# A two-layer decoder step on one core: four conditioning items of the second layer move from the first layer's route into the sparse attention, whose eight groups are reordered

## What is computed

```python
def ada_mod(c, w, b):
    return jnp.split(jax.nn.silu(c) @ w + b, 6, axis=-1)
...
for i in range(DEPTH):
    sh1, sc1, gt1, sh2, sc2, gt2 = ada_mod(c, w_ada[i], b_ada[i])
    h = modulate(x, norm_mix[i], sh1, sc1)          # rms_norm * (1 + scale) + shift
    m = gla_mixer(h, ...) if i % 2 == 0 else dsa_mixer(h, ...)
    x = x + gt1 * m
    x = x + gt2 * moe_ffn(modulate(x, norm_ffn[i], sh2, sc2), ...)
```

```python
logits = einsum('btkgd,btskd->btkgs', qg, k_sel) * ATT_DH ** -0.5
p = softmax(where(valid, logits + bias, -inf))
o = einsum('btkgs,btskd->btkgd', p, v_sel)
```

## Time and profile before

| | |
|---|---|
| median of 3 runs | 1783.02 us (1780.09 to 1785.51) |
| profiled execution | 1780.96 us |
| its span | 1779.1 us |
| TensorE busy | 1624.9 us (91%), mean granted clock 0.959 |
| VectorE, ScalarE, GpSimd busy | 709.7, 442.2, 166.5 us |
| moved by transfers | 552.37 MB, mean 310 GB/s |

### The profile page before, as it was taken

How to read it: one execution, slowest core, us unless ns; L and a number is a source line. 1 busy time by engine, 2 the same in 40 slices (tenths; PEclk the granted TensorE clock), 3 DMA queues, 4 the chain that set the end, 5 groups by cost and what they waited for, 6 DMA issues and landing times. The chain is left out here.

```text
span 1779.1 us, 30764 instructions
## 1 busy us (share of the span) xinstructions
PE 1624.9 (91%) x11629; PEld 971.7 (55%) x11756; DVE 709.7 (40%) x1909; ACT 442.2 (25%) x985; POOL 166.5 (9%) x229
## 2 busy tenths in 40 slices
PE   5999898899999999999988957798999999999997
PEld 4687475455555555555456744575555555455554
DVE  3123536055333333333332775245733333333334
ACT  2110112122222222222231114131222222222223
POOL 0000300000000000000010424001000000000000
PEclk9899699799999999999999969799999999999999
DMA  9875644999999999999771412065999999999990
GB/s 362 326 259 172 213 148 168 409 385 383 415 416 417 416 414 413 413 416 415 280 297 33 143 49 60 1 239 215 391 402 416 416 416 416 413 416 416 413 396 30
DMA packets 139031, 552.37 MB, mean 310 GB/s; under 512 B 19407, under 2 KB 36637, under 8 KB 104662
## 3 DMA queue, kind: packets, MB, share of 16 engines
q1 hardware_dynamic: 120562, 513.82, 72.5%
q0 software_dynamic: 15392, 34.66, 5.6%
q10 hardware_dynamic: 3012, 3.00, 0.5%
HBM read 562.74 MB, written 8.60 MB: 321 GB/s over the span
## 5 line engine op out<-in xcount | busy, mean ns | idle before, releaser
L1316 PE MATMUL PS<-ring,arena 128*64 128x256 f32 x4288 | 490.7, 382 | 2.5 <-ACT arena L1633 1.5
L1316 PEld LDWEIGHTS PS<-ring,arena 128*64 128x64 f32 x4288 | 304.2, 137 | 182.6 <-issue 41.0
L1340 PE MATMUL PS<-ring,arena 128*64 128x512 f32 x1072 | 259.6, 605 | 1.4 <-ACT arena L1618 1.4
L1540 DVE TENSOR_TENSOR arena<-arena,PS 128x128 f32<-128x128 f32 x134 | 38.6, 288 | 373.9 <-ACT arena L1616 367.9
L1279 PE MATMUL PS<-arena 128*128 128x512 bf16 x669 | 169.4, 384 | 15.1 <-issue 9.2
L1524 DVE TENSOR_SCALAR arena<-arena 128x512 bf16<-128x512 f32 x130 | 62.7, 483 | 256.5 <-ACT arena L1627 256.5
L1626 ACT COPY arena<-PS 64x512 f32<-64x512 f32 x134 | 77.5, 578 | 301.9 <-PE PS L1340 301.9
L1340 PEld LDWEIGHTS PS<-ring,arena 128*64 128x64 f32 x1072 | 65.1, 136 | 120.4 <-issue 104.0
L1646 POOL COPY arena<-arena 128x1 int32 (+1 forms) x71 | 14.5, 204 | 1187.7 <-PE PS L1270 972.0
L1279 PEld LDWEIGHTS PS<-arena 128*128 128x128 bf16 (+1 forms) x796 | 69.6, 99 | 91.5 <-issue 27.7
L1616 ACT ACTIVATE arena<-PS 128x128 f32<-128x128 f32 x134 | 37.2, 278 | 326.4 <-PE PS L1316 326.4
(11 more groups left out here) (482 smaller groups left out, 1618.4 us busy)
## 6 DMA issues: line engine op xcount, KB each, us to landing
ring<-in_moe_w_gate SPq DMA_DIRECT2D x134, 1024.0 KB, 7.8
ring<-in_moe_w_up SPq DMA_DIRECT2D x134, 1024.0 KB, 10.3
ring<-in_moe_w_down SPq DMA_DIRECT2D x134, 1024.0 KB, 15.4
ring<-in_w_ada SPq DMA_DIRECT2D x32, 1152.0 KB
ring<-in_w_ada SPq DMA_DIRECT2D x16, 768.0 KB
ring<-in_gla_w_in SPq DMA_DIRECT2D x8, 1152.0 KB
ring<-in_dsa_w_in SPq DMA_DIRECT2D x6, 1024.0 KB
arena<-in_state_gla POOLq DMA_DIRECT2D x8, 512.0 KB, 5.8
```

The costliest lines, as they stand in the source:

```text
L1316: m = pe.matmul(PS[64 * half:64 * half + 64, 5, 0:256].rearrange("p (g n) -> p g n", g=2), rows[:, k, CAP * b:CAP * b + CAP], gu[:, :, k, ...
L1340: m = pe.matmul(PS[64 * j:64 * j + 64, 7, :], hTt[b][:, kk * CAP:(kk + 1) * CAP], ring[:, s, 2, kk * D + 512 * j:kk * D + 512 * j + 512], ...
```

## The change

Items 4 to 7 of layer 1 leave `pe_route(0)`. Items 4 and 5 have their columns (`pe_late_rows`) behind the first logits of the sparse attention, item 6 behind the transposes of the seventh group, and item 7 at the start of `pe_route(1)`, in place of the seven warming products. Their folds, copies and additions have new functions (`pe_late_fold`, `act_late_rows`, `dve_late`); the rows between lie in `hT` or, for item 7, in its own ring slot. The ring's plan has new slots and a new order: items 5, 6 and 7 are loaded ahead of `w_out`, and the gathers of keys and values use slots that items 4 and 5 had. In the attention, a third buffer for a group, a double one for maximum and sum, a bank of its own for each half-wide group, and a new order: on TensorE logits of `it + 1`, mix of `it - 1`, transposes of `it`; on VectorE scale and mask of `it`, normalising of `it - 1`, maximum of `it`; on ScalarE exponential of `it + 1`, copy of `it`. The prefix sum stands ahead of the transposes of keys and values. The column of a sample's own key is appended to its turned keys by a second copy, so that one product of 257 columns takes the place of one of 256 and one of 1. `Osel` is made on all partitions by 4 operations instead of 16, without the memset.

```diff
-        it_ada[1] = plan(8, at=after)
-        it_ex = [plan(NE, False, at=after[2:] + after[:2] + [it_sh[0][0]]), None]
+        it_ada[1] = plan(4, at=after)
+        it_ex = [plan(NE, False, at=after[1:] + after[:1] + [it_sh[0][0]]), None]
...
+        sa, sb_, sc_, sd = [it_ex[0][u][0] for u in (2, 3, 0, 1)]
+        it_dsa = plan(3, at=[sa, sb_, sc_])
+        hold_raw = hold(sd)
+        it_ada[1] += plan(4, at=[sa, sd, sb_, sc_])
+        hold_k = hold(sa)
+        hold_v = hold(sd)
+        it_dout = plan(2, at=[sb_, sa])
+        it_sh[1] = plan(1, at=[sd])[0]
+        it_ex[1] = plan(NE, False, at=[sb_, sc_, sa, sd])
...
+        def pe_late_rows(i, b):
+            s, _ = it_ada[1][i]
+            item_ready(pe, it_ada[1][i])
+            for t in range(3):
+                for kk in range(2):
+                    for g in range(4):
+                        m = pe.matmul(PS[32 * g:32 * g + 32, b + t // 2, 256 * (t % 2):256 * (t % 2) + 256],
+                                      cT[:, 2 * g + kk, :], wide(s)[:, 2 * g + kk, 256 * t:256 * t + 256],
+                                      start=(kk == 0), stop=(kk == 1), skip_group_check=True)
+            m.then_inc(S("late_rows"), 1)
+            pe.wait_ge(S("late_rows"), i - 3)
+            if i < 7:
+                pe.sem_inc(S(f"slot_used{s}"), 1)
+        def pe_late_fold(i, b, c0):
+            pe.wait_ge(S("mod_rows"), 9 + i)
+            for j in range(6):
+                m = pe.matmul(PS[:, b, c0 + 16 * j:c0 + 16 * j + 9], late_rows(i)[:, j // 2, P * (j % 2):P * (j % 2) + P], K["fold"],
+                              start=True, stop=True)
+            m.then_inc(S("mod_fold"), 1)
...
         def pe_route(l):
-            pe_warm(7)
+            if l:
+                pe_late_rows(7, 5)
+            else:
+                pe_warm(7)
...
             turn_h(0)
+            if l:
+                pe_late_fold(7, 7, 256)
...
-                for i in range(8):
+                for i in range(4):
                     pe_ada_rows(1, i, 3 * (i % 2))
...
+            dve_at(pe, "gteq")
+            pe.matmul(PS[:, 0, 0:2], lowtri, gteq, start=True, stop=True)
+            pe.matmul(PS[:, 0, 2:3], K["m16"], gteq[:, 0:1], start=True, stop=True).then_inc(S("dsa_pe"), 1)
             pe.wait_ge(S("relu"), IH)
...
+            logits(0)
+            pe_late_rows(4, 4)
+            pe_late_rows(5, 6)
+            for it in range(8):
+                if it < 7:
+                    logits(it + 1)
+                if it < 2:
+                    pe_late_fold(4 + it, 5 + 2 * it, 256)
                 if it >= 1:
+                    mix_values(it - 1)
+                if it == 4:
+                    pe.wait_ge(S("mod_T"), 14)
+                turn_probs(it)
+                if it == 6:
+                    pe.wait_ge(S("logit_sb"), 8)
+                    pe_late_rows(6, 0)
+            mix_values(7)
+            pe_late_fold(6, 5, 0)
...
-                    pe.matmul(PS[:, 0, 0:256], Qs[:, Pq, b * P:(b + 1) * P], KTs[b % 4][:, Pq, :], start=(b == 0 and Pq == 0), stop=False, skip_group_check=True)
-                    m = pe.matmul(PS[:, 0, 256:257], Qs[:, Pq, b * P:(b + 1) * P], kT[:, Pq, SEQ + b:SEQ + b + 1], start=False, stop=False, skip_group_check=True)
+                    m = pe.matmul(PS[:, 0, 0:257], Qs[:, Pq, b * P:(b + 1) * P], KTs[b % 4][:, Pq, :], start=(b == 0 and Pq == 0), stop=False, skip_group_check=True)
...
             for it in range(8):
+                masked(it)
+                if it >= 1:
+                    normed(it - 1)
+                largest(it)
+                if it in (1, 2):
+                    dve_late(3 + it, 3 + 2 * it, 256)
+            normed(7)
...
-            dv(dve.memset(Osel, 0.0))
...
             for kv in range(KVH):
+                dst = Osel.rearrange("p (b c d) -> p b c d", b=2, c=2)[:, :, 0]
+                src = PS[:, 1, :].rearrange("p (b k d) -> p k b d", b=2, k=KVH)[:, kv]
...
+            for it in range(8):
+                if it < 7:
+                    exps(it + 1)
+                if it == 4:
+                    mixed_out(0)
+                probs_out(it)
+                if it == 6:
+                    act_late_rows(6, 0)
+            mixed_out(1)
...
             sp_dsa()
+            sp_ada(1, [5, 6, 7])
             sp_dout(0)
             sp_dout(1)
```

More of the change, by code:

```diff
@@ L1478, in dve_route @@
             if l == 0:
-                dve_ada(1)
+                dve_ada(1, range(4))
         def dve_over(l):
@@ L1696, in build @@
         m8 = tk(2, 8)
-        nm, rs, mx = tk(4), tk(4), tk(4)
+        nm, rs = [tk(4) for _ in range(2)], [tk(4) for _ in range(2)]
+        mx = tk(4)
         mxn = tk(4)
@@ L1740, in build @@
         selfP = X2[:, 1300:1308]
[L1741 removed]
+        KTs = [X3[:, 514 * i:514 * i + 514].rearrange("p (q n) -> p q n", q=2) for i in range(4)]
         DC = {k: mrow[:, o:o + w] for k, (o, w) in DSAC.items()}
@@ L1986, in pe_dsa @@
-            pe.wait_ge(S("att_o_sb"), 2)
+                if it >= 2:
+                    pe.wait_ge(S("logit_sb"), it if T else it - 1)
+                r = slice(64 * (kv % 2), 64 * (kv % 2) + 64)
+                for g in range(4):
+                    dst = PS[:, g // 2, 256 * (g % 2):256 * (g % 2) + 2 * P] if T else PS[:, it % 2, P * g:P * g + P]
+                    pe.matmul(dst, qT[r, (kv // 2) * 4 + g, T * P:(T + 1) * P], kT[r, kv // 2, 0:P * (T + 1)],
+                              start=(g % (2 if T else 4) == 0), stop=False, skip_group_check=True)
@@ new lines, in mix_values @@
+            def mix_values(it):
+                T, kv = it // 4, it % 4
+                pe.wait_ge(S("p_T_sb"), it + 1)
+                if it == 4:
+                    pe.wait_ge(S("att_o_sb"), 1)
+                for g in range(4):
+                    ft = kv * 2 + g // 2
+                    for st in range(T + 1):
+                        m = pe.matmul(PS[64 * (g % 2):64 * (g % 2) + 64, 2 + ft // 4, (ft % 4) * P:(ft % 4 + 1) * P],
+                                      vtk[:, st, kv * 64:(kv + 1) * 64], PTs[it % 2][:, st, g, :], start=(st == 0), stop=(st == T))
+                m.then_inc(S("pv"), 1)
@@ L2171, in dve_dsa, with masked @@
-            dve.wait_ge(S("att_o_sb"), 2)
+            def masked(it):
+                T = it // 4
+                n = P * (T + 1)
+                if it >= 3:
+                    dve.wait_ge(S("p_T"), it - 2)
+                dve.wait_ge(S("asc"), it + 1)
+                src = PS[:, 0:2, :].rearrange("p b (g n) -> p (b g) n", g=2) if T else bank(it % 2).rearrange("p (g n) -> p g n", g=4)
+                dve.scalar_tensor_tensor(out=A2[it % 3][:, :, 0:n], in0=src, scalar=DH ** -0.5, in1=bc(sw[:, P * T:P * T + n], 1, 4),
+                                         op0=ALU.mult, op1=ALU.add).then_inc(S("logit_sb"), 1)
@@ L2319, in _ @@
             sp_moe(0)
-            sp_ada(1)
+            sp_ada(1, range(4))
             sp_experts_first(0)
@@ L2385, in _ @@
             act_route(0)
-            act_ada(1)
+            act_ada(1, range(4))
             act_experts(0)
```

154 lines of the change are left out of this document (77 added, 77 removed).

## The result

The changed kernel takes 1754.37 us (median of 4 runs, 1752.76 to 1760.55), the kernel before 1781.55 us on the same chip (median of 4, 1779.28 to 1785.51). The ratio is 0.9845, 95% interval 0.9826 to 0.9863: 27 us faster, 1.5%. I had predicted 1741 with a range of 1732 to 1752, so the direction was right and about 13 us of the gain are missing. The profiled execution took 1755.12 us, its span is 1753.3.

What follows compares the result with a forecast made beforehand. First route bound by transfers, expert loops by TensorE, sparse attention by a chain across engines. Terms -31.1 - 2.7 + 0.9 - 3.4 - 4.3 + 0.6 = -40.0 from 1780.96 gave 1741 us, range 1732 to 1752.

Steps and rivals of the forecast that it cites:

- Term 1: First route: four conditioning items leave it, so the shared down projection starts earlier and no new wait appears; -31.1 us.
- rivals C and D: C: first experts wait for loads, 1757, chance 0.04. D: later key and value gathers, slower, 1798 at 2.4 times, chance 0.02.
- Term 2: Selection: prefix sum ahead of the key and value transposes, so VectorE goes on earlier; -2.7 us.
- Term 3: Eight attention groups, reordered, with three items among them: wide groups 7.7 us apart, up to the sample queries +0.9 us.
- rival A: Eight attention groups: TensorE's gaps let the clock fall, or ScalarE's copies hold the transposes; about +6, 1747 us; chance 0.20.
- the sign that I had named: Eight attention groups: the prediction is wrong if the groups stand more than 9 us apart.
- Term 4: Sample logits: one product of 257 columns in place of 256 and 1; -3.4 us.
- Term 5: Osel made on all partitions by four operations in 1.6 us instead of 16; -4.3 us.
- rival B: Late items hide wholly (-4) and the output projection starts warm (-3.3): 1734 us; chance 0.18.
- Term 6: Second route: item 7's columns stand in for seven warming products, its copies and fold mostly hidden; +0.6 us.

Runs made afterwards that it cites:

- the fill: Changed kernel plus ten warming products in the first gap: 1747.05 us; with three more ahead of the transposes of groups 4, 5 and 6: 1744.72 us.
- the run with the small edits: Kernel before with only the prefix sum ahead of the transposes, 257 columns in one product and four Osel operations: 1768.14 us, ratio 0.9907.
- the run with early items and the order of before: Changed kernel with items 4 and 5 folded before the selection ends, second logits held until the first masking step, groups in the old order: 1741.36 us.

## Why the prediction was too fast

**Term 1** (-31.1): measured -30.2 at L1253. No transfer wait came in its place, and TensorE waits for `ring` nowhere behind the first route, so rivals C and D did not occur.

**Term 2** (-2.7): right, VectorE's wait ahead of its step fell from 4.50 to 1.68 us. Another 1.0 came from what I had not counted: the product that follows ran at the full clock, 1.32 us against 2.29; TensorE had stood 2.64 us ahead of it where it had stood 4.80, and the clock fell only at 1004.0, as it ended.

**Term 3** (+0.9): this is the step that failed; measured +17.8 (+18.1 and -0.3). I wrote "TensorE's gaps in the new cycle (1.7 us in 7.7)" under rival A and "gaps of that length exist now" against it, and I costed the cycle of the wide groups at the full clock. The cycle was right: 7.66 measured for 7.7 where the clock was up, but the sign that I had named, groups more than 9 us apart, was there. What I missed is what the edit does at the front. Before, the second logits waited for the first masking step and filled the time in which ScalarE and VectorE do the first softmax (1059.60 to 1063.7); TensorE was at the lower level then as well, after its 9.70 us, but came back with this work. I saw in them only work that could go ahead. Moved ahead, they leave 5.04 us empty, and the clock stays low for 27 us. Rival A had the mechanism, but priced two groups at the lower level and +6; five of the seven intervals were lengthened (8.55 to 10.97 us). With the fill, 10.1 of the 18.1 us come back at the front hole and 3.2 at the later gaps; 4.7 remain against the order of before, of which about 3 are the last low stretch (9.88 where its neighbours have 6.2 and 7.67). That the low clock made the groups slow is shown; why it came back after 4.9 us of work in the kernel before and only after 23.6 here is not.

**Term 4** (-3.4): the size was right, 3.3 where the clock is up (12.12 us in the run with the small edits). In the changed kernel it was -0.7, as the clock was low from 1093 to 1103; TensorE's longest pause in the 5 us before that was 1.10 us, so what lowered it is open. The 15.44 of before is itself one execution: the same kernel took 18.3 in the other.

**Term 5** (-4.3): measured -4.3, four operations in 1.55 us. The gap ahead of the output projection shrank, and the first column came 1.5 us sooner: so much of the 3.3 that rival B put on it did occur.

**Term 6** (+0.6): measured +0.3.

The Trainium skill, "TensorE: Matmul & The Clock Gate", section "What's actually happening", says that the low clock is the default and activity releases it. The trace agrees on the fall behind the wait of 5.04 us, and on the recovery only in part: from 1028.2 to 1043.4 TensorE was busy 14.61 of 15.20 us by the profile and stayed at 0.50. By that rule alone, read with the profile's busy share, the full clock would have been expected back.

## What to carry to other kernels

When an edit moves work of TensorE ahead of the wait it used to fill, ask what TensorE does in that wait now: here, filling a hole of some 5 us gave 10 us back, because the work behind it had run at 1.2 GHz. The length of a hole does not tell its price, though: the kernel before stood for 9.70 us just ahead of its second logits and lost far less, so read the clock behind the hole. Hold spare work back with a wait so that it falls into the hole; a place in the queue alone does not put it there. And look at the queues of the other engines: copies for the extra work must not stand ahead of the softmax that ends the hole.

## What the runs showed of the hardware

- A TensorE that the profile shows busy does not always get its full clock back: 14.61 of 15.20 us busy at 0.50 in the changed kernel. In the kernel before it was back after 4.9 us of work, and in the run with early items and the order of before 5.4 us after the first masking step. What differs between them I have not separated; in one place (the sample logits of the kernel before) two executions of the same kernel differed, 10 us low in one and 17 in the other.
- The clock can fall after TensorE has started again: in the run with item 5 moved, transposes (0.66 us) and logits (1.16 us) behind a hole of 3.39 us still ran at the full clock. And it can fall with no long pause ahead: the longest in the 10 us before was 1.13 us in the run with early items and the order of before.
- Warming products cost nothing where they fit: with ten in the hole the transposes stood 5.82 us behind the first masking step (5.81 without them) and the step fell from 58.16 to 48.03 us; with twenty they stood 9.50 behind it, and the step was 51.10.
- Waits with the releaser "remote" (0.8 to 2.6 us each) come and go between executions of one kernel, and move a stage by 3 us.
